# The order of the attention steps in a two-layer hybrid decoder: halves of projection groups, silu by token tile, stores on another queue

## What is computed

```python
h = _rmsnorm(x, norm_attn)
z = h @ w_in
gq, gk, gv, ga, gg, sq, sk, sv = jnp.split(z, _SPLITS, axis=-1)
g = jax.nn.log_sigmoid((ga @ w_gk2 + b_gk2).astype(f32)) / GATE_NORMALIZER
o, S = _gla(q, k, v, g.reshape(B, T, GLA_HEADS, GLA_DK), S0.astype(f32))
o = _rmsnorm(o, gla_norm) * jax.nn.silu(gg.reshape(B, T, GLA_HEADS, GLA_DV).astype(f32))
qs = _rope(sq.reshape(B, T, SWA_HEADS, SWA_HEAD_DIM), pos)
ks = _rope(sk.reshape(B, T, SWA_KV_HEADS, SWA_HEAD_DIM), pos)
o_swa, kc, vc = attend(qs, ks, vs, sinks)          # softmax over a window of 128, with a sink
x = x + jnp.concatenate([o_gla, o_swa.astype(x.dtype)], axis=-1) @ w_o
h = _rmsnorm(x, norm_ffn)
x = x + (jax.nn.silu(h @ w_gate) * (h @ w_up)) @ w_down
```

## Time and profile before

| | |
|---|---|
| time, median of 3 runs (lowest to highest) | 2448.18 us (2447.93 to 2450.8) |
| time of the profiled execution, and its span | 2446.66 us, 2444.9 us |
| TensorE busy | 2341.1 us, 96% of the span |
| VectorE, ScalarE, GpSimd busy | 58%, 35% (865.8 us), 1112.6 us |
| mean granted clock of TensorE | 0.983 |

### The profile page before, as it was taken

One profiled execution on the slowest core, in us unless ns is written; L12 is line 12 of the kernel. 1 busy time (PEld: TensorE's weight loads), 2 busy tenths in 40 slices (PEclk: granted clock), 3 DMA queues, 4 the chain that ended last, 5 costly groups with the idle time before them and its releaser, 6 DMA issues.

```text
span 2444.9 us, 43787 instructions
## 1 busy us (share of the span) xinstructions
PE 2341.1 (96%) x16240; PEld 2239.5 (92%) x16240; DVE 1419.6 (58%) x2828; ACT 865.8 (35%) x1964; POOL 1112.6 (46%) x1415
## 2 busy tenths in 40 slices
PE   6999899999999999999999998999999999999997
PEld 5886788999999999999998777899999999999997
DVE  5746575356555555555675666653665555555556
ACT  4136555352222222222431454553322222222224
POOL 5210101435656666666651111025366666666665
PEclk9999998999999999999999999989999999999999
DMA  3300102111111111111231001021111111111112
GB/s 139 133 27 27 44 18 73 61 36 35 53 53 53 52 44 45 53 52 53 71 124 48 32 18 44 20 88 44 44 53 53 45 53 45 52 37 51 53 52 89
DMA packets 47325, 132.35 MB, mean 54 GB/s; under 512 B 4288, under 2 KB 21888, under 8 KB 46336
## 3 DMA queue, kind: packets, MB, share of 16 engines
q1 hardware_dynamic: 38208, 110.91, 13.6%
q10 hardware_dynamic: 8928, 18.71, 2.1%
HBM read 117.18 MB, written 14.45 MB: 54 GB/s over the span
## 4 chain that ended last, share of the span: by engine, by line
PE 87%; DVE 4%; ACT 3%; issue 3%; POOL 2%; SPq 0%; DMA 0%; DVEq 0%; POOLq 0%; ACTq 0%; PEldq 0%
PE acc L754 17%; PE acc L755 16%; PE acc L756 16%; PE pair_a L754 6%; PE pair_a L755 6%; PE pair_a L756 6%; PE single L755 3%; PE single L756 3%; PE single L754 3%; PE pair_a L936 1%; PE single L919 1%; ACT prob_t L1315 1%; PE acc L986 1%; PE single L973 1%; POOL root_row L666 1%
## 5 line engine op out<-in xcount | busy, mean ns | idle before, releaser
L704 POOL TENSOR_TENSOR w_lo<-w_raw,w_hi 128x256 fp32r<-128x256 f32 x480 | 377.9, 811 | 431.1 <-ACT w_hi L1461 431.1
L643 POOL TENSOR_TENSOR w_lo<-w_raw,w_hi 128x256 fp32r<-128x256 f32 x264 | 206.8, 814 | 729.0 <-ACT w_hi L1145 729.0
L754 PE MATMUL acc<-h_hi,w_hi 128*128 128x384 f32 (+1 forms) x1200 | 409.4, 341 | 27.7 <-DVE h_lo L1625 9.4
L755 PE MATMUL acc<-h_lo,w_hi 128*128 128x384 f32 (+1 forms) x1200 | 397.6, 331 | 0.0
L756 PE MATMUL acc<-h_hi,w_lo 128*128 128x384 f32 (+1 forms) x1200 | 396.4, 330 | 0.0
L1461 ACT ACTIVATE w_hi<-w_raw 128x512 fp32r<-128x512 f32 x240 | 151.2, 630 | 535.4 <-PE single L756 347.3
L754 PEld LDWEIGHTS acc<-h_hi,w_hi 128*128 128x128 f32 x1200 | 233.3, 194 | 45.9 <-DVE h_lo L1625 11.8
L754 PE MATMUL acc<-f_hi,w_hi 128*128 128x264 f32 (+2 forms) x896 | 260.6, 291 | 12.3 <-issue 7.7
L755 PE MATMUL acc<-f_lo,w_hi 128*128 128x264 f32 (+2 forms) x896 | 258.6, 289 | 0.0
L756 PE MATMUL acc<-f_hi,w_lo 128*128 128x264 f32 (+2 forms) x896 | 258.2, 288 | 0.0
L755 PEld LDWEIGHTS acc<-h_lo,w_hi 128*128 128x128 f32 x1200 | 233.7, 195 | 0.1
(11 more groups left out here) (299 smaller groups left out, 6319.1 us busy)
## 6 DMA issues: line engine op xcount, KB each, us to landing
w_raw<-units SPq DMA_DIRECT2D x186, 512.0 KB, 3.4
park<-x ACTq DMA_DIRECT2D x2, 2640.0 KB, 16.4
x<-park ACTq DMA_DIRECT2D x2, 2640.0 KB, 8.7
y_t<-x SPq DMA_DIRECT2D x4, 768.0 KB, 3.5
rope<-tables SPq DMA_DIRECT2D x2, 1056.0 KB, 7.2
s<-state_in ACTq DMA_DIRECT2D x4, 512.0 KB, 5.0
state_s<-s SPq DMA_DIRECT2D x2, 1024.0 KB, 5.1
x<-x_t SPq DMA_DIRECT2D x2, 768.0 KB, 5.7
```

What stands on the lines that cost most here:

```text
L643: low = nc.gpsimd.tensor_tensor(w_lo[:, s, a:a + LOW], w_raw[:, s, a:a + LOW], w_hi[:, s, a:a + LOW].bitcast(f32), ALU.subtract)
L704: low = nc.gpsimd.tensor_tensor(w_lo[:, s, b:b + LOW], part[:, a:a + LOW], w_hi[:, s, b:b + LOW].bitcast(f32), ALU.subtract)
L754: nc.tensor.matmul(out, wh, hi, start=first, stop=False, skip_group_check=resumed)
L755: nc.tensor.matmul(out, wh, lo, start=False, stop=False, skip_group_check=resumed)
```

## The change

The same instructions are issued in another order. Six things move:

1. A projection group can be issued in two halves of four feature chunks (`zh`, then `z`), with other steps between; the bank is opened by the first half.
2. In the loop over items the order is `norm_p n-1`, `scores n`, `values n-2`, first half of a group, `turn_p n-1`, second half, `take`, `exp_p n`, and then what went along with the group (gates, turned values). One group goes to each item, and two groups and two half groups are kept for later.
3. For the sampled tokens `dec_scores` stands one group later, `dec_norm` ahead of a take, and `dec_values` between two halves.
4. At the start of the gated part the kept groups lie between the first exponentials and the first scores.
5. At the end silu, gating and splits go by token tile, and the first halves of the first output projection unit (those that need only the softmax heads) are issued ahead of them. The sampled states move up by two groups.
6. The small stores are issued by SyncE, ahead of its loads of units 9 (`U_GK + 3`) and 22 (`U_WO + 3`).

```diff
@@ schedule
-    steps += [("turn_k",)] + rest[0]
+    def halved(item, between):
+
+        return [("zh",) + item[0][1:], *between] + item
+
+    steps += [("turn_k",)] + rest[0] + rest[1]
+    done = 2
     for g in range(2):
-        a, b, c = rest[1 + 3 * g:4 + 3 * g]
-        steps += [("dec_scores", g)] + a + b + [("dec_norm", g), ("dec_turn", g)] + c + [("dec_values", g)]
+        a, b, c = rest[done:done + 3]
+        steps += [("dec_scores", g)] + a + [b[0], ("dec_norm", g)] + b[1:] + [("dec_turn", g)]
+        steps += halved(c, [("dec_values", g)])
+        done += 3
     items = 2 * NCH
-    first = done = 7
+    first, last = done, len(rest) - 2
     for n in range(items + 1):
+        upto = first + (last - first) * (n + 1) // (items + 1)
+        batch = rest[done:upto]
+        done = upto
+        if n > 0:
+            steps.append(("norm_p", n - 1))
         if n < items:
             steps.append(("scores", n))
-        if n > 0:
-            steps.append(("norm_p", n - 1))
         if n > 1:
             steps.append(("values", n - 2))
-        upto = first + (len(rest) - first) * (n + 1) // (items + 1)
-        half = done + (upto - done + 1) // 2
-        for r in rest[done:half]:
-            steps += r
-        if n > 0:
-            steps += [("turn_p", n - 1)]
-        for r in rest[half:upto]:
-            steps += r
-        done = upto
+        item = batch[0]
+        taken = [s[0] for s in item].index("take") + 1
+        steps += halved(item[:taken], [("turn_p", n - 1)]) if n > 0 else item[:taken]
         if n < items:
             steps.append(("exp_p", n))
+        for r in [item[taken:]] + batch[1:]:
+            steps += r
...
-    steps += exponents(0) + exps(0) + project(*gate[0]) + decays(0) + exponents(1) + exps(1)
+    steps += exponents(0) + exps(0) + rest[last] + halved(project(*gate[0])[:1], rest[last + 1])
+    steps += decays(0) + [("take",) + gate[0]] + exponents(1) + exps(1)
...
+    steps += project(*gate[11]) + [("zh", U_WO, tt) for tt in range(NTT)]
+    steps += [("silu", hd, 0) for hd in gla] + [("split", k, 2) for k in swa] + [("gate_out", hd, 0) for hd in gla]
+    steps += [("split", k, 0) for k in gla] + [("round", U_WO + 1)]
+    for tt in range(1, NTT):
+        for hd in gla:
+            steps += [("silu", hd, tt), ("gate_out", hd, tt)]
+        steps += [("split", k, tt) for k in gla]
+    steps.append(("unpark",))
+    for tt in range(NTT):
+        if tt == NTT - 1:
+            steps.append(("sample_states",))
+        steps += project(U_WO, tt) + [("split_x", 0, tt)]
@@ sync
+                    if u == U_GK + 3:
+                        g = GROUPS[l][("turn_k",)]
+                        sp.wait_ge(S.acc_free[g % ACCS], g // ACCS + 1)
+                        sp.dma_start(kc_p[l, 0], kno[:, 0, :]).then_inc(S.out_sem, 16)
...
+                    if u == U_WO + 3:
+                        sp.wait_ge(S.s_ready, NCH)
...
                     sp.wait_ge(S.w_ready, u - RING + 1)
                     load(l, u)
@@ tensor
-                        for k in order:
+                        mine = order
+                        if (u, tt) in parted:
+                            mine = order[:KC // 2] if s[0] == "zh" else order[KC // 2:]
+                        for k in mine:
@@ vector, first decays
                         if c == 0:
                             left(dve, S, GROUP[("z", U_GA, NTT - 1)])
-                            left(dve, S, GROUP[("turn_v", U_GG - 1, NTT - 1)])
...
                         else:
+                            left(dve, S, GROUP[("turn_v", U_GG - 1, NTT - 1)])
                             link(nc.vector.memset(qpads, 0.0))
```

More of the change, by code:

```diff
@@ L191, in schedule @@
             steps.append(("gla_stat", c - 1))
-        steps += [("take",) + gate[c + 1], ("gla_state", c), ("gla_out", c), ("gla_state_sum", c)]
+        steps += [("take",) + gate[c + 1], ("gla_state", c)]
+        if c == NCH - 1:
+            steps.append(("gla_rstd", c - 1))
+        steps += [("gla_out", c), ("gla_state_sum", c)]
         if c + 2 <= NCH:
             steps += exps(c + 2)
-        if c > 0:
+        if 0 < c < NCH - 1:
             steps.append(("gla_rstd", c - 1))
-    steps += [("sample_scores",), ("gla_square", NCH - 1), ("gla_scale", NCH - 2)] + project(*gate[9])
@@ L198, in schedule @@
[L198 to L205, removed]
@@ L206, in schedule @@
-    steps += [("gate_out", GH - 1), ("split", GH - 1, 0), ("unpark",)]
-    steps += [("split", k, tt) for tt in range(1, NTT) for k in mixed]
-    for k in range(KC):
+    swa, gla = range(GH, KC), range(GH)
+    steps += [("z",) + gate[9], ("gla_square", NCH - 1), ("sample_scores",), ("take",) + gate[9], ("gla_scale", NCH - 2)]
+    steps += halved(project(*gate[10])[:1], [("gla_stat", NCH - 1), ("gla_rstd", NCH - 1), ("sample_out",)])
+    steps += [("split", k, 0) for k in swa] + [("gla_scale", NCH - 1), ("gla_square", NCH), ("take",) + gate[10]]
@@ new lines, in schedule @@
+    steps += [("gla_stat", NCH)] + [("split", k, 1) for k in swa] + [("gla_rstd", NCH), ("gla_scale", NCH)]
+    steps += project(*gate[11]) + [("zh", U_WO, tt) for tt in range(NTT)]
[5 more added lines that the diff above has]
+        steps += [("split", k, tt) for k in gla]
@@ L210, in schedule @@
+    steps.append(("unpark",))
[3 more added lines that the diff above has]
+        steps += project(U_WO, tt) + [("split_x", 0, tt)]
+    for k in range(1, KC):
         for tt in range(NTT):
             steps += project(U_WO + k, tt) + [("split_x", k, tt)]
-            if k == 1 and tt == 0:
-                steps.append(("sample_states",))
             if k == 2 and tt == 0:
@@ L218, in schedule @@
         out.append(s)
-        if s[0] == "take" and s[1] >= U_SQ and s[2] == NTT - 1:
+        if s[0] == "take" and s[1] >= U_SQ and s[2] == NTT - 1 and s[1] != U_WO - 1:
             out.append(("round", s[1] + RING))
@@ L347, in trunk, with counted @@
     assert all(n == G_FF for _, n in numbered)
-    SPLIT = {s: n for n, s in enumerate(s for s in STEPS[0] if s[0] == "split")}
+    def counted(kind):
+        return {s: n for n, s in enumerate(s for s in STEPS[0] if s[0] == kind)}
+    SPLIT, SILU, GATED = counted("split"), counted("silu"), counted("gate_out")
     ORDER = [[b for n in range(2) for b in ((n, *kt) for kt in blocks(l, n))] for l in range(DEPTH + 1)]
@@ L768, in _ @@
                 S, GROUP, steps = L[l], GROUPS[l], STEPS[l]
+                parted = {s[1:] for s in steps if s[0] == "zh"}
                 def open_group(g):
@@ L794, in _ @@
                         last.then_inc(S.head_full, 1)
-                    elif s[0] == "z":
+                    elif s[0] in ("zh", "z"):
                         _, u, tt = s
[L797 to L800, removed]
+                        g = GROUP[("z", u, tt)]
+                        order = range(KC) if u < U_WO else [*range(GH, KC), *range(GH)]
+                        if s[0] == "zh" or (u, tt) not in parted:
+                            open_group(g)
+                            if tt == 0:
+                                pe.wait_ge(S.w_ready, u + 1)
                         out = bank(g)[:, 0:width(tt)]
-                        order = range(KC) if u < U_WO else [*range(GH, KC), *range(GH)]
-                        for k in order:
+                        mine = order
+                        if (u, tt) in parted:
+                            mine = order[:KC // 2] if s[0] == "zh" else order[KC // 2:]
+                        for k in mine:
                             if u == U_WO:
```

64 lines of the change are left out of this document (31 added, 33 removed).

## The result

The changed kernel took 2462.99 us (median; 2459.0 to 2465.76), the kernel before 2448.38 us beside it: 1.0058 times as long, 95% interval 1.0045 to 1.0072. It is slower by 14.6 us; 2470 was forecast, with a range of 2452 to 2488. The profiled execution took 2459.0 us with a span of 2457.0, 12.1 above the span before. An edit moves these lines by up to 15; the tiles tell the steps apart in every run: `pair_b <- DVE prob` is the turn waiting for the division, `single <- ACT prob_t` the values waiting for the copy, `acc <- DVE h_lo` of the last stage the output projection waiting for the splits.

A forecast was written before the change was run, and what follows sets the result against it. Bound: TensorE's waits, 19.7 us in the second layer's attention, and the clock after them. Per layer 17.5 + 5.4 - 0.7 - 3.2 - 5.4 - 2.6 = +11 us, +22 for both: 2470 us, range 2452 to 2488.

The forecast's parts named there:

- The loop of gate items: Prompt attention, items 5 to 10: scores, exponentials, gate and division run serially, 10.7 us each, 65.2 in sum; TensorE waits 19.1.
- The turn's wait: Sign in the changed profile: TensorE's turn waiting for the division grows from 2.1 to some 22 to 26 us per layer.
- the order of scores and division: Item loop: dividing item n-1 ahead of the scores of item n leaves no overlap; called the term that decides.
- Rounding: Items 0, 3, 12 and 15: weight-unit rounding waits for the group's end and delays the exponentials, together 7.0 us.
- a gain of 6.5 at the values: Second layer's prompt attention: turning between halves removes the 6.5 us the values wait for ScalarE's copy.
- The clock in the gate items: Gate items: the clock falls in every second one, 3 x 1.8 = +5.4 us per layer, bounds 0 and 10.8.
- a fall behind 2.5 us: Evidence from the earlier profile: a layer 0 stretch with a 2.5 us wait had a mean clock of 0.77.
- Rival 3: Gate items: the clock falls in all six, 5.4 us more per layer, 2481 us; chance 0.22.
- Sampled tokens: Turns of the sampled tokens: division ahead of the last group's take removes both waits, -3.2 us per layer.
- Start of the gated part: First gated scores: wait of 1.4 us for 4.0 and the clock stays, -5.4 us per layer.
- End: End of attention, work by token tile: -1.9 us and -0.7 for the clock per layer; second tile's splits 2 us late.
- Stores: Small stores moved from ScalarE to SyncE, 7.7 us of issues per layer: 0 effect; +6 if the loads' cover is gone.

The follow-up runs named there:

- the best version: Changed kernel with gates behind the next item's scores, rounding behind the exponentials, sampled tokens' states ahead of the second tile's output projection: 2397.74 us, 0.9801.

## Why the prediction held, and where it was off

*The loop of gate items: right, in mechanism and size.* I put six turns at 65.2 us without the clock's share; they took 65.5 with one slow one. The chain of rows above runs as forecast (10.34 for 10.7), with VectorE's scan directly ahead of the division and ScalarE's gate directly behind the exponentials. That the sums agree within 0.3 us is luck: the slow item is 2.7 us longer than forecast, and the other five are 2.3 us shorter together. The turn's wait of 20.0 lies just under the 22 to 26 forecast. The difference is in item 6, where TensorE's work at half the clock took 11.6 us for 7.1 and filled what would have been wait. Moving the gates took 14.6 us per layer back.

*What the prediction blamed was wrong.* It says that the order of scores and division decides. The runs show otherwise: with scores first and the rest as changed the kernel takes 2536 us. No one edit is the cause; each order closes a loop of its own with the gates' new place. With scores first, gates behind the turn put TensorE into the loop, and moving them ahead of the turn took 33 us off. With division first, gates ahead of the exponentials changed nothing, gates behind the next scores took 29 us off, and whole groups alone 17. Where the gates stand behind turn and exponentials, division first is the better order. The text named the gates' place as one fact of the loop and never asked what the loop would be with the other order and the gates left there.

*Rounding: 7.0 forecast, 6.0 of waits seen, 6.5 returned.* Right. But I booked the halves as a gain of 6.5 at the values alone, and did not see that whole groups would have kept the rounding out of the way: without halves and nothing else moved, the kernel is 17 us faster.

*The clock in the gate items: the term that was mis-sized.* Three falls at 1.8 us were put down, 5.4 per layer. There was one, in each layer, and the item behind it took 12.97 for a forecast of 10.3: 2.7 us. The other five items were 0.4 to 0.6 us shorter each than forecast, 2.3 in all. Over two layers these make 10 us, more than the 7 between forecast and median; the end gave some of it back. The row of before on which I leaned, a fall behind 2.5 us, did not carry over: 2.48 and 3.01 us passed at 1.00 here. The earlier trace rows held a warning: the stretch from 1425, at 0.84, has no wait longer than 1.1 us. Rival 3 took every waiting turn to start at the low rate. The Trainium skill, "TensorE: Matmul & The Clock Gate", section "HAM oscillation — how this bites in real kernels", tells this of a loop that waits some 3 to 5 us for a transfer in every turn. The six waits here are 1.4 to 3.7 us, two of them over 3 us, and the clock fell at one of these two.

*Sampled tokens: 3.2 forecast, 3.9 seen.* From the turn of the keys to the first scores the layers take 44.4 and 45.9 us for 44.0 and 45.5, though a group of 4.3 us more lies there. The turns have no wait left.

*Start of the gated part: 5.4 forecast, 5.6 seen.* The wait is 1.2 for 4.0 and the clock stays at 1.00; from the first gated scores to the last gated output 75.2 us for 78.1 and 78.0.

*End: 2.6 forecast; 2.8 in the first layer, a loss of 0.5 in the second.* The second tile's splits came 3.5 us late for the 2 that I took, and the clock fell there for 17 us in the second layer, through the states of the sampled tokens. The run that moved these states shows that the cover was there to be had, one step later in the order.

*Stores: 0, and 0 was measured.*

Sum of the changed stages as the two traces show them: in the first layer -3.9 + 16.5 - 5.7 - 2.8 = +4.1, in the second -3.9 + 15.0 - 5.6 + 0.5 = +6.0, where 16.5 and 15.0 are the item loop, from the first scores to the first gated scores, with the moved group added and the shorter wait at its end taken out. With 1.7 us in the feed-forward parts and 0.5 ahead of the first layer this is 12.3, against 12.1 between the spans. The forecast had 11 for each layer, with 22.2 for the loop: 2.7 of the difference there is the clock, 2.3 the five shorter items, 1.0 the rounding.

## What to carry to other kernels

When steps that lie on several engines share one written order, write down the loop that each order closes, with every engine in it, and price all the orders and not only the one at hand: here the order, the halves, the gates' place and the rounding's gave 2413 to 2536 us in their combinations. Work of a second kind, such as the gate here, can go where each of its engines waits for another: behind the scores it cost least, and the best of the places tried depended on the order. Splitting a group to hide a copy also delays what waits for the group's end, so look for that first.

## What the runs showed of the hardware

The length of a wait alone does not tell whether the granted clock falls. With the gates behind the next scores, and nothing else moved, the turn of item 6 waits 3.1 us in both layers; the stretch around it has a mean clock of 0.91 in the first and 1.00 in the second, and the item behind it takes 9.8 us and 8.3:

```profile
195.00:215.00 20.00, 16.90 (x96) 13.01 (x96) 15.81 (x29) 12.71 (x34) 2.94 (x4) 0.91 0.08 27
1385.00:1405.00 20.00, 16.87 (x107) 12.93 (x107) 16.17 (x29) 13.05 (x35) 2.94 (x4) 1.00 0.09 27
```

The clock also falls where TensorE has not waited. In the changed kernel it is at half from 1599.3 us, behind 32 products of 8 columns each for the sampled tokens, with TensorE busy throughout:

```profile
1595.00 3.74 PE L1055 MATMUL single<-qz,s 128*128 128x8 f32 x32
1599.30:1602.70 3.40, 3.40 (x14) 3.40 (x13) 3.09 (x6) 2.07 (x7) 0.00 (x0) 0.50 0.02 5
```

A fall costs time even where TensorE waits in the loop anyway: behind the fall at 1397.9 the turn took 1.97 us for 1.09, the gate's product came later, and the loop was 2.7 us longer than forecast, of some 4.5 us that the half rate added to TensorE's work in that item. In the best version the clock stays at 1.00 through all of the second layer's item loop.
